# A decoder layer on one core: the MLP's modulation vectors formed earlier, one weight split on another engine, two unused products

## What is computed

```python
h = h + g1[:, None, :] * (y_mix @ w_out)                 # residual 1
hn2 = _modulate(_rmsnorm(h, norm_ffn), sh2, sc2)         # per row 1/rms, then * (1+sc2) + sh2
up = _causal_dwconv(hn2 @ w_up, conv_w, conv_b)          # w_up: 1024 x 5632
gate, val = up[..., :D_FF], up[..., D_FF:]
h = h + g2[:, None, :] * ((gelu(gate) * val) @ w_down)   # residual 2
```

## Time and profile before

| | |
|---|---|
| median of 3 runs | 763.49 us (762.62 to 764.20) |
| the profiled execution | 754.84 us, of which the span from first to last instruction is 753.0 us |
| mean granted TensorE clock | 0.981 of full |
| TensorE matmul busy | 700.5 us, 93% of the span |
| VectorE busy | 460.3 us, 61% |
| ScalarE busy | 338.7 us, 45% |
| GpSimd busy | 271.2 us, 36% |

### The profile page before, as it was taken

How to read it: one execution, slowest core, us unless ns; L and a number is a source line. 1 busy time by engine, 2 the same in 40 slices (tenths; PEclk the granted TensorE clock), 3 DMA queues, 4 the chain that set the end, 5 groups by cost and what they waited for, 6 DMA issues and landing times.

```text
span 753.0 us, 9891 instructions
## 1 busy us (share of the span) xinstructions
PE 700.5 (93%) x3566; PEld 555.1 (74%) x3566; DVE 460.3 (61%) x811; ACT 338.7 (45%) x508; POOL 271.2 (36%) x216
## 2 busy tenths in 40 slices
PE   0899999998887899999699999999999999999997
PEld 0587777777674566888697888888878887888886
DVE  2868987976989789798725757645544455000005
ACT  4534446756422646523566454555544554122120
POOL 2002899229816100000204443443442442443440
PEclk9999999999879999999899999999999999999999
DMA  9952221260371647654603233223223223223302
GB/s 336 375 143 67 76 93 57 95 186 0 46 77 45 202 179 277 247 203 166 237 17 112 59 109 111 85 82 111 81 86 112 84 84 112 92 76 111 110 3 111
DMA packets 63080, 91.46 MB, mean 121 GB/s; under 512 B 12010, under 2 KB 41474, under 8 KB 62979
## 3 DMA queue, kind: packets, MB, share of 16 engines
q1 hardware_dynamic: 59520, 89.44, 37.1%
q10 hardware_dynamic: 3523, 1.54, 0.7%
HBM read 86.28 MB, written 4.69 MB: 121 GB/s over the span
## 4 chain that ended last, share of the span: by engine, by line
PE 67%; DVE 23%; issue 4%; ACT 3%; POOL 1%; DMA 1%; SPq 0%; ACTq 0%; DVEq 0%; POOLq 0%
PE bank L1597 20%; PE bank L1599 20%; PE bank L1598 20%; DVE arena L1176 4%; DVE arena L1152 2%; DVE arena L1313 2%; DVE w_lo L1162 2%; PE bank L1602 2%; DVE stat L1310 2%; PE bank L1946 1%; DMA xh<-in_x 1%; DVE stat L1101 1%; PE bank L1941 1%; DVE up L1496 1%; DVE arena L1369 1%
## 5 line engine op out<-in xcount | busy, mean ns | idle before, releaser
L504 POOL TENSOR_TENSOR w_lo<-w_raw,w_hi 128x2048 fp32r<-128x2048 f32 x34 | 156.8, 4612 | 345.1 <-ACT w_hi L700 178.7
L1597 PE MATMUL bank<-act_hi,w_hi 128*128 128x512 f32 (+2 forms) x384 | 147.7, 385 | 5.6 <-DVE act_lo L1534 4.0
L1598 PE MATMUL bank<-act_lo,w_hi 128*128 128x512 f32 (+2 forms) x384 | 146.5, 382 | 0.0
L1599 PE MATMUL bank<-act_hi,w_lo 128*128 128x512 f32 (+2 forms) x384 | 146.5, 381 | 0.0
L1597 PE MATMUL bank<-w_hi,act_hi 128*128 128x512 f32 x240 | 98.5, 411 | 1.0 <-DVE act_lo L1202 1.0
L1599 PE MATMUL bank<-w_hi,act_lo 128*128 128x512 f32 x240 | 94.9, 396 | 0.0
L1598 PE MATMUL bank<-w_lo,act_hi 128*128 128x512 f32 x240 | 94.6, 394 | 0.0
L1597 PEld LDWEIGHTS bank<-act_hi,w_hi 128*128 128x128 f32 x384 | 73.0, 190 | 20.5 <-issue 4.8
L700 ACT ACTIVATE w_hi<-w_raw 128x2048 fp32r<-128x2048 f32 x26 | 49.7, 1913 | 84.6 <-PE bank L1599 81.8
L1549 DVE SCALAR_TENSOR_TENSOR conv<-bank,vec_cols,conv 128x511 f32<-128x511 f32 x44 | 33.0, 749 | 83.2 <-ACT conv L1058 82.8
L1598 PEld LDWEIGHTS bank<-act_lo,w_hi 128*128 128x128 f32 x384 | 73.1, 190 | 14.3 <-issue 0.2
(11 more groups left out here) (318 smaller groups left out, 1180.3 us busy)
## 6 DMA issues: line engine op xcount, KB each, us to landing
w_raw<-in_w_up SPq DMA_DIRECT2D x44, 512.0 KB, 4.7
arena<-in_w_ada SPq DMA_DIRECT2D x18, 1024.0 KB, 8.5
w_raw<-in_w_down SPq DMA_DIRECT2D x22, 512.0 KB, 3.9
w_raw<-in_w_in SPq DMA_DIRECT2D x10, 1024.0 KB, 5.2
xh<-in_x SPq DMA_DIRECT2D x8, 512.0 KB, 7.3
w_raw<-in_w_out SPq DMA_DIRECT2D x4, 1024.0 KB, 10.2
arena<-in_w_ada SPq DMA_DIRECT2D x2, 2048.0 KB, 10.7
arena<-lag_dram SPq DMA_DIRECT2D x16, 128.0 KB, 5.6
```

The costliest lines, as they stand in the source:

```text
L504: nc.gpsimd.tensor_tensor(w_lo[:, slot, 0:width], w_raw[:, slot, 0:width], w_hi[:, slot, 0:width].bitcast(F32), ALU.subtract).then_inc(S[" ...
L1597: T.matmul(dst, lhs_hi, rhs_hi, start=start, stop=False)
L1598: T.matmul(dst, lhs_hi, rhs_lo, start=False, stop=False)
L1599: return T.matmul(dst, lhs_lo, rhs_hi, start=False, stop=stop)
```

## The change

`mod2_ready` is formed by DVE ahead of `rstd_of_h((0, 1, 2))`, not behind `mixed(1, 3)`. ACT takes `square_h(1, 3)` behind `modulate(1)` and `hi(U_UP+1)`, and waits for `h_ready` 8 between `modulate(0)` and `modulate(1)`, since `mixed(1, 3)` on DVE uses the half of `up32` that `modulate(1)` writes. The low part of unit `U_UP+1` is formed by DVE behind `hn_lo(1)`, not by POOL. The row factor of tile 3 is formed behind `hn_lo(2)` and applied behind `modulate(3)`. PE gets two products of the identity with `gate1_row`, 128x512 in float32, whose results nobody reads: one ahead of the wait for `hn`, one ahead of the first product of `up_first`. `turn_last_hn(0)` goes behind block 5, not block 4.

```diff
@@ gpsimd
-            pool.wait_ge(S["lo_ready"], U_UP + 1)
-            pool.wait_ge(S["hi_ready"], U_UP + 2)
-            lo(slot(U_UP + 1))
+            pool.wait_ge(S["lo_ready"], U_UP + 2)
@@ scalar
             scale_h(1)
-            square_h(1, 3)
             act.wait_ge(S["mod2_ready"], 1)
...
+                if k == 0:
+                    act.wait_ge(S["h_ready"], 8)
                 if k == 1:
                     hi(U_UP + 1)
-                if k == 2:
+                    square_h(1, 3)
+                if k == 3:
                     scale_h(3)
@@ vector
             for t in range(3):
                 mixed(1, t)
-            rstd_of_h((0, 1, 2))
-            for t in (0, 2):
-                signal(V.tensor_scalar(hn[:, t, :], xh[:, t, :], rstd_h[:, t:t + 1], None, ALU.mult), "hn_even")
-            mixed(1, 3)
             dve.wait_ge(S["ada_sum_ready"], 1)
...
             link(V.scalar_tensor_tensor(scale2, scale2, 1.0, vec_cols[:, C_NFFN:C_NFFN + KD], ALU.add, ALU.mult),
                  "mod2_ready")
+            rstd_of_h((0, 1, 2))
+            for t in (0, 2):
+                signal(V.tensor_scalar(hn[:, t, :], xh[:, t, :], rstd_h[:, t:t + 1], None, ALU.mult), "hn_even")
+            mixed(1, 3)
...
                 if k == 1:
+                    lo(U_UP + 1)
+                if k == 2:
                     rstd_of_h((3,))
@@ tensor
+                pe.wait_ge(S["h_ready"], 4)
+                T.matmul(bank[7][:], ident[:], gate1_row[:, 0:512], start=True, stop=True)
                 pe.wait_ge(S["hn_even"], 2)
                 pe.wait_ge(S["hn_ready"], 1)
                 for k in range(3):
                     turn_hn(k)
                 pe.wait_ge(S["h_ready"], 8)
+                T.matmul(bank[3][:], ident[:], gate1_row[:, 0:512], start=True, stop=True)
...
-                    if k == 4:
+                    if k == 5:
                         pe.wait_ge(S["hn_ready"], 2)
                         turn_last_hn(0)
```

## The result

Three sets of runs of the changed kernel were timed, each beside runs of the kernel before. Their ratios to before, with 95% intervals, are 0.9941 (0.9914 to 0.9969; medians 759.28 and 762.59 us, 20 runs each), 0.9986 (0.9950 to 1.0021; 759.98 and 759.93) and 0.9950 (0.9913 to 0.9986; 757.80 and 761.46). Weighted by the inverse squares of the intervals' widths they give 0.9956, with an interval of 0.9937 to 0.9975: **some 3.4 us faster, 1.9 to 4.8**. These ratios leave out the changed kernel's slow runs (765.09, 765.50 and 766.74 us, and one of 1952.03), though the kernel before reached 766.55 without any being left out; from plain means with the first three counted, the same weighting gives 0.9964 (0.9947 to 0.9981), 2.8 us faster. The forecast was 4.0 us and 759.5.

The account below looks back on a forecast made before the run. PE's waits between 359 and 402 us, from the residual into `up_first`, were taken as the bound. 1.41 + 1.57 + 1.91 - 0.26 - 0.62 - 0.03 = 3.98; 763.49 - 4.0 = 759.5 us, range 758.2 to 761.9.

Parts of the forecast that it names:

- what block 4 gains arrives at the end whole: Behind block 4 of `up_first`: PE does the same products without a gap up to the 1.6 us pause; 4.0 us carried over.
- the sign of being wrong altogether: Behind block 4: the forecast would be wrong altogether if PE's time there were not the same as before.
- The stretch: From the residual into `up_first`: block 4 at 375.0 us, not 378.98, 4.0 us earlier.
- the second unused product was over in time: Ahead of block 0: it ends by 364.2, before block 0 at 364.33, hidden by 0.1 us.
- Scale and shift cost nothing: DVE's two `mod_cols` instructions fit its idle 0.79 us before 357.74; without that cover they cost 0.4 us.
- second rival: Tile 3's row factor: POOL did not cause the long step, or DVE stands still otherwise; 0.3 us lost, 763.8; chance 0.05.
- first rival: Transposes and block 0: the clock falls all the same; only 2.2 us gained, 761.3; chance 0.15.
- third rival: Loops: shifted code makes them stall each turn for instructions; 6.4 us over 10 turns of `up(j)`, 765.9; chance 0.02.
- 1.41: Start of block 0: at 364.33 us, 1.41 us earlier, as ACT's first modulation waits only for three transposes.
- 1.57: Block 0: the unused products keep full clock, so it costs 2.44 us instead of 4.01, 1.57 less.
- 1.91: Ahead of block 2: the late start removed, 372.19 to 374.10, 1.91 us.

Follow-up runs that it names:

- fill_only: The kernel before with the two unused products alone; block 4 at 17.18 us after the first transpose, nothing gained; no timed ratio given.

## Why the prediction was wrong, and where it was right

**Wrong: that what block 4 gains arrives at the end whole.** This is the step that failed. The prediction took the 1.6 us pause ahead of the loop as a chain that moves with PE's work, put no term on the clock there, and carried the 4.0 us over to the end as they were. The chain did move with it: the pause is 1.58 us in the profiles before and after. The clock did not keep. In two of three profiles of the changed kernel it fell to 0.50 at that pause, for 6.8 and 3.4 us, and the products of the loop came 2.77 and 1.36 us later; in the first profile of before, from which the prediction was made, it had held. The prediction named this as the sign of being wrong altogether, PE's time behind block 4 not being the same as before, and it was not: 351.88 us from the loop to the end of the span, then 354.97. The profiled execution thus came to 756.0 us and not to the forecast's 750.9: 1.9 from work ahead of the change, 2.8 from this fall, 0.3 from the slower pace in the loops, of which the prediction had no term either. On the median it cost less, as the kernel before pays there too in some executions: 3.4 of 4.0 us arrived (2.8 by the plain means), and whether the missing part is that loss or scatter the intervals don't tell.

What decides whether the clock falls at a pause stays open. Its length alone does not: pauses of 1.54, 1.66 and, in `fill_only`, 3.23 us kept the clock, and one of 1.58 lost it in six profiles and kept it in five. This one stands behind tile 3's products of 128 columns, which start every 0.11 us, the others among products of 384 columns or ahead of transposes; whether that matters was not tried.

**The stretch: right, step by step.** Block 4 at 13.18 us from the first transpose against 13.2 forecast (375.0 less 361.78), the same in all three profiles. Its parts: block 0 at 2.63 (2.55 forecast; the second unused product was over in time, PE waited 0.19 for VectorE's low part), 2.44 us for it at full clock, block 2 at 7.77 (7.69), block 3 at 10.74 (10.75). Scale and shift cost nothing, covered by 0.57 us left of the wait for the square. No step on `stat` is long, and two experiments moved the standstill to other instructions of VectorE, each of which ended with GpSimd's or within 0.42 us of it: the second rival is out. With the unused products the clock held through the nine transposes in all seven profiles that have them, and without them it fell in all six others: the first rival is out. The rule of the Trainium skill ("TensorE: Matmul & The Clock Gate", Part 4) that transposes do not count as other products do would have made the nine transposes no cover; the clock of the 359.00 to 380.00 row, 1.00, held all the same, with unused products on both sides of them. Whether the transposes themselves counted, no run shows. The third rival, loops that stall for their instructions, is out as well: PE has no idle time behind the loop's first product in any profile, and the slower pace of 0.3 to 0.8 us is found in the kernel before too.

**Missed: that before has no fixed price.** The stretch took 39.34, 39.34 and 40.92 us in three profiles of the kernel before, since the clock fell behind the wait ahead of block 2 in the third (1.95 us there, 1.66 and 1.58 in the others). One execution could not show that. The change removes this wait, and its stretch is the same to 0.02 us in all profiles.

**The sum as a list of terms.** The stretch's total was right, but its terms, 1.41, 1.57 and 1.91, are no prices of the parts of the change. The unused products alone gained 0.0, the split alone 0.8, the early scale and shift alone less than nothing; together 4.0. Two waits stood in a row, on PE's clock and on VectorE's chain, and each part shortens one side only. The prediction's text works block by block along the later of the two, which is why its total held; a reader who added the terms for a part of the change would have been wrong, as the three single experiments show.

**Range and chances.** 759.5 with 758.2 to 761.9 took in the medians 759.28 and 759.98, not the third, 757.80: the range was made as if the measurement were certain. The kernel before itself was measured at 763.49, 762.59, 759.93 and 761.46.

## To carry to other kernels

Work along the chain from a mark inside the kernel (here the first transpose) and compare stretches between marks: the changed stretch repeated to 0.02 us in the changed kernel, where the total scattered by more than 10. When a stretch gets shorter, look at each pause that is left behind it, its length and what the engine did ahead of it, and put a term on the clock there, or try it with the pause taken away or filled, before counting the gain; where two chains wait for each other, change both ends at once, since either alone may bring nothing. VectorE and GpSimd should not both be given work with two inputs in SBUF while one of them is on the path: VectorE's small step stood still for up to 4.50 us here.

## What the runs showed of the hardware

- VectorE's instructions with both inputs in SBUF, however small, stood still while GpSimd's subtraction over two SBUF tiles ran: a step on 128x1 numbers took 4.50 and 4.10 us, one on 128x384 3.36, against 0.15 and 0.56 alone, each ending 0.02 to 0.42 us behind GpSimd's. VectorE's convolution steps, with one input in PSUM, took 0.75 us beside the same instruction of GpSimd.
- The granted clock fell at the same pause of 1.58 to 1.59 us in some executions and not in others, of unchanged code, six of eleven profiles, and stayed low for 3.4 or 6.8 us. A pause of 3.23 us elsewhere left it at 1.00.
- With the same code up to some 350 us, the kernels reached the first transpose at 361.78 to 369.73 us in the thirteen profiles. The low stretches of the clock ahead of it differ in number and length; that they are the whole of that scatter is not shown.
- The same products, at a granted clock of 1.00 and without idle time of PE, took 0.6 to 0.8 us longer over some 150 to 190 us in some executions than in others: the first 150 us of the loops took 0.60 us more in the third profile after than in the first before, and in `fill_only` 0.78 us were added between 157 and 347 us. The cause is open.
